# An FFN's wide gate and up groups on TensorE: contraction tiles outside and product kinds inside, or the other way round

## The reference, cut to what matters

```
def swiglu(x, w_gu, w_dn):
    g, u = jnp.split(x @ w_gu, 2, axis=-1)
    return (jax.nn.silu(g) * u) @ w_dn
...
        h = h + swiglu(rmsnorm(h, norm_ffn[l]), w_gate_up[l], w_down[l])
```

## Time and profile before

| | |
|---|---|
| time, median of 3 runs | 2611.77 us (2611.46 to 2612.14) |
| the profiled execution's own time | 2613.04 us |
| its span, first to last instruction | 2611.3 us |
| TensorE (PE) busy, 15296 matmuls | 2575.4 us, 99% |
| weight loads (PEld) busy, 15296 | 2511.1 us, 96% |
| VectorE, ScalarE, GpSimd busy | 1107.2, 673.1, 675.1 us |
| mean granted TensorE clock | 0.996 |

### The profile page before, as it was taken

How to read it: one execution, slowest core, us unless ns; L and a number is a source line. 1 busy time by engine, 2 the same in 40 slices (tenths; PEclk the granted TensorE clock), 3 DMA queues, 4 the chain that set the end, 5 groups by cost and what they waited for, 6 DMA issues and landing times. The chain is left out here.

```text
span 2611.3 us, 37891 instructions
## 1 busy us (share of the span) xinstructions
PE 2575.4 (99%) x15296; PEld 2511.1 (96%) x15296; DVE 1107.2 (42%) x2301; ACT 673.1 (26%) x1474; POOL 675.1 (26%) x641
## 2 busy tenths in 40 slices
PE   8999999999999999999999999999999999999998
PEld 7999999999999999999999988899999999999998
DVE  6444464254323333332338656655333233333334
ACT  5222233142111111111115555534111111111112
POOL 1322222212221211122126343434121112211114
PEclk9999999999999999999999999999999999999999
DMA  4445555111111111111112234011111111111111
GB/s 148 142 133 143 166 172 165 49 33 41 49 41 41 42 41 48 33 49 41 41 61 42 55 81 119 18 41 49 41 43 42 46 33 49 44 42 45 41 41 73
DMA packets 244240, 171.23 MB, mean 66 GB/s; under 512 B 47352, under 2 KB 232876, under 8 KB 244036
## 3 DMA queue, kind: packets, MB, share of 16 engines
q1 hardware_dynamic: 243876, 168.78, 22.2%
q10 hardware_dynamic: 192, 0.04, 0.0%
HBM read 136.99 MB, written 33.59 MB: 65 GB/s over the span
## 5 line engine op out<-in xcount | busy, mean ns | idle before, releaser
L197 POOL TENSOR_TENSOR wl<-raw,wh 128x512 fp32r<-128x512 f32 x264 | 337.6, 1303 | 1288.4 <-ACT wh L189 1288.4
L349 PE MATMUL psum<-xh,wl 128*128 128x400 f32 (+1 forms) x1872 | 430.1, 338 | 0.0
L349 PE MATMUL psum<-xl,wh 128*128 128x400 f32 (+1 forms) x1872 | 428.5, 337 | 0.0
L349 PE MATMUL psum<-xh,wh 128*128 128x400 f32 (+1 forms) x1872 | 427.3, 336 | 0.0
L477 DVE TENSOR_TENSOR h<-h,psum 128x384 f32<-128x384 f32 (+1 forms) x528 | 265.0, 553 | 280.0 <-PE psum L369 267.2
L349 PEld LDWEIGHTS psum<-xh,wl 128*128 128x128 f32 x1872 | 336.7, 188 | 0.0
L349 PEld LDWEIGHTS psum<-xl,wh 128*128 128x128 f32 x1872 | 336.6, 188 | 0.0
L349 PEld LDWEIGHTS psum<-xh,wh 128*128 128x128 f32 x1872 | 335.9, 188 | 0.0
L2201 PE MATMUL psum<-xh,wh 128*128 128x384 f32 (+1 forms) x792 | 276.6, 349 | 8.0 <-DVE h L2373 4.8
L2201 PE MATMUL psum<-xl,wh 128*128 128x384 f32 (+1 forms) x792 | 272.2, 344 | 0.0
L2201 PE MATMUL psum<-xh,wl 128*128 128x384 f32 (+1 forms) x792 | 270.9, 342 | 0.0
(11 more groups left out here) (248 smaller groups left out, 3698.0 us busy)
## 6 DMA issues: line engine op xcount, KB each, us to landing
raw<-in_w_gate_up SPq DMA_DIRECT2D x88, 512.0 KB, 3.9
raw<-in_w_down SPq DMA_DIRECT2D x44, 512.0 KB, 3.5
raw<-in_a_w_in SPq DMA_DIRECT2D x24, 512.0 KB, 4.8
fr_qkv<-qkv_d SPq DMA_DIRECT2D x36, 256.0 KB, 3.8
qkv_d<-fr_tmp SPq DMA_DIRECT2D x32, 192.0 KB, 2.0
hn_d<-fr_hn_turned SPq DMA_DIRECT2D x36, 128.0 KB, 3.3
fr_xin<-in_x_prompt SPq DMA_DIRECT2D x8, 512.0 KB, 5.3
fr_decode_state<-in_state_c SPq DMA_DIRECT2D x4, 1024.0 KB, 7.2
```

The costliest lines, as they stand in the source:

```text
L197: pool.tensor_tensor(wl[:, self.slot(p), v], raw[:, self.raw_of(p), v], wh[:, self.slot(p), v].bitcast(F32), ALU.subtract).then_inc(self.w ...
L349: y = pe.matmul(psum[:, bank + c, 0:nt], w[:, k, :], x[:, k, t0:t0 + nt], start=(k == 0 and m == 0), stop=(k == KD - 1 and m == 2))
```

## The change

The loops over `k` and over the three kinds change places in `gate_up_wide`. The chunk stays the innermost loop. All 72 matmuls of a group are the same ones as before, with the same operands, banks, first and last accumulation flags and increments.

```
--- before.py
+++ after.py
@@ -343,8 +343,8 @@
         def gate_up_wide(p, bank):
             pe.wait_ge(self.w_lo, self.z["w_lo"] + 2 * (p + 1))
             hi, lo = weight_tile(wh[:, self.slot(p), :]), weight_tile(wl[:, self.slot(p), :])
-            for k in range(KD):
-                for m, (w, x) in enumerate(((hi, xh), (hi, xl), (lo, xh))):
+            for m, (w, x) in enumerate(((hi, xh), (hi, xl), (lo, xh))):
+                for k in range(KD):
                     for c, (t0, nt) in enumerate(tok):
                         y = pe.matmul(psum[:, bank + c, 0:nt], w[:, k, :], x[:, k, t0:t0 + nt],
                                       start=(k == 0 and m == 0), stop=(k == KD - 1 and m == 2))
```

## The result

The changed kernel takes 2619.05 us (median of 9 runs), the one before 2611.46 us in the same rounds: a ratio of 1.0029, with a 95% interval of 1.0019 to 1.0038. The change makes the kernel slower by 7.6 us. The forecast was 2615.0 us within 2609 to 2623. The time lies in the range. Its ratio is over the bound of 0.2% that I had drawn for "no difference" (the interval begins just under it, at 0.19%), so it lies in the field of the rival to which I had given 0.33.

What follows compares the result with a forecast made beforehand. TensorE, busy without gaps at full clock in the wide groups, was taken as the bound. Steps of k in layer 1 (+2.3 us) and layer 0 (+0.9) made +3.2 us, so 2615.0 us on the 2611.8 median, range 2609 to 2623.

Steps and rivals of the forecast that it cites:

- the rival to which I had given 0.33: Line 349's matmuls run at the narrow gate groups' rate: +7.0 and +5.9 us, 2624.7 us; layer 1 alone 2618.8; chance 0.33.
- What bounds the kernel: In both stretches of wide groups TensorE is always busy at full clock, so each nanosecond of a matmul counts.
- Waits, increments, loads: Wide groups: waits and increments keep their places, other engines have slack, no weight load is added or removed; no cost.
- One sign of being wrong: The forecast would be wrong if, among other signs, the down projections changed their time too; 25.22 and 25.38 us were expected.
- The stationary tile: Wide groups: eight more tile changes at 5.5 ns would make 3.4 us over 78 groups; this price was not taken.
- Steps of k, layer 1: Layer 1's wide groups: sixteen more steps of k at 3.6 ns cost 58 ns a group, +2.3 us; bounds -1.1 to +7.0.
- Layer 0: Layer 0's wide groups: +3.4 us if steps of k cost, -1.7 if column jumps do; the middle, +0.9 us, taken.
- The sum: Both layers' wide groups together: 2.3 + 0.9 = +3.2 us, giving 2615.0 us, +0.12%.
- The comparison with N / 2.4 + 2.5 ns: For 384 columns the formula gives 162.5 ns against 173.3 to 176.2 in the trace, leaving some 11 ns a matmul.
- The two ports: TensorE reads columns and weight loads independently, so loads take nothing from running matmuls; cited for the no-difference side, chance 0.22.
- the rival without any effect: Read order in wide groups makes no difference, 2611.8 us, or the excess goes entirely, 2609.0 us; chance 0.22.
- P: Follow-up explanation, not in the forecast: a matmul is held up when its columns' start address modulo 256 bytes changes.

Runs made afterwards that it cites:

- the kinds innermost: Against the kernel before: k outside, then the chunk, then the kinds inside, so the stationary tile changes at 48 of 72 matmuls; 2615.46 us in one execution.
- the place outside: Against the change: loops over the columns' start address modulo 256 bytes outermost, then kind, then k = a and a + 4, then chunk; 2613.84 us, ratio 1.0009.

## Why the prediction was right or wrong

**What bounds the kernel** was right. TensorE has no gap in the two stretches, and each nanosecond between starts reached the end: 6.8 us of longer groups are 6.8 us of span.

**Waits, increments, loads** at no cost: right. No wait appeared in the two stretches, counts and load times stayed. One sign of being wrong that the prediction had named did come, in small: the wide down projections of layer 1 changed their time, by 15 ns each.

**The stationary tile** at no price: right for layer 1, and the kernel with the kinds innermost showed it directly. The 5.5 ns worked out from narrow and wide groups was the price of something else in which these differ.

**Steps of k, layer 1**: the mechanism was right and its size wrong. The term was +2.3 us, and it measured 6.25 us. The step that failed is the choice among the three bounds: "the wide form is nearer in all but that one point". That one point, a step of `k` every three matmuls, was the one that counted. I had the row with the same rhythm and named it as the upper bound; groups behind another group came to within 0.1 ns a matmul of it. I had priced every step alike, at 3.6 ns. A step cost (12.507 - 12.480) / 8 = 3.4 ns in the old order and (12.680 - 12.480) / 24 = 8.3 ns in the new one.

The steps aren't alike even within a group. At the floor three matmuls take 520 ns. In the old group the three triples behind each of four places in a row differ from that by -5.0, 0, 0; -4.2, +12.5, +2.5; -3.4, 0, 0; and +10.8, 0, 0 ns, in all 13 ns, and the next four places repeat it. In the new group, one triple to a place, it is +10.9, +1.7, +17.4 and +3.3 ns, 33 ns for four places, six times over. That the next place comes before the rhythm has settled fits this, but it isn't shown as the reason. In the old order with `xl` moved by 64 bytes the place moves 16 times, at distances of three and six matmuls, and a move costs 53 / 16 = 3.3 ns, no more than in the old layout. With the place outside the rhythm doesn't settle within 18 matmuls: behind one of the four moves the six triples are off by +5.4, +4.9, +2.4, +1.5, +5.1 and +6.0 ns.

**Layer 0**: the middle of +3.4 and -1.7 was +0.9, measured +0.4 us. The number is near, but neither of the two rules behind it held: a group in the steady run has the same 12.680 us in both orders, and the 0.4 us stands at the ten groups behind a down projection. That is luck more than insight.

**The sum**: +3.2 us, measured +6.8 in the span and +7.6 between the medians, whose interval reaches from 0.19 to 0.38%. The rival "behaves as the narrow gate groups do", for layer 1 alone, had 2618.8 us and was the right one. I should have given it more than the forecast. The comparison with N / 2.4 + 2.5 ns in the prediction leaves something out: the Trainium skill (TensorE: Matmul & The Clock Gate, "Back-to-back issue gap") gives that formula for isolated matmuls and says that in a stream of weight loads and matmuls both set the spacing. So the 11 ns by themselves don't speak against it.

**The two ports.** By the Trainium skill (TensorE: Matmul & The Clock Gate, "Step-by-step: what each phase is for") the columns and the weight loads are read through two independent ports, so that a load takes nothing from a running matmul. Nothing in layer 1 speaks against that: 48 changes of the tile in a group and not 16 left it at 12.507 us. What failed is my step from there to "the order makes no difference". The rule says nothing of the start address of the columns, and by order and layout the same 72 matmuls took 12.480 to 12.680 us.

**What stays open.** Shown is that in the gate, up and wide down groups of layer 1 the time over the floor comes with changes of the columns' place modulo 256 bytes: where the place was held constant, groups behind one another ran at the floor, the gate and up groups in either order. Not shown is why, nor what a change costs. Over the floor, a wide group paid 200 ns for 24 changes, 53 for 16, 40 for 12, 27 for 8, 60 for 4 and 20 for 2, so the number of changes doesn't give the price.

Nor does every change cost. The narrow down projection of the earlier trace rows reads hidden tiles whose parts lie 36 x 256 + 128 bytes apart with rows of 18 x 256 + 64 bytes. Counted from the first one, its place modulo 256 bytes goes 0, 128, 0, 64, 192, 64, another at every matmul, and it runs at 173.3 ns all the same (in layer 1 too: 1.040 us for six by the starts, where nothing comes between). The wide down projection of layer 1 reads the same tiles with three matmuls at each place and took 257 ns over its floor. The prediction had named this row as speaking for the rival without any effect, and P as stated above doesn't explain it.

I can't say either which hardware resource it is, why the place outside was slower than the old order, or what sets layer 0's times, where a chunk of 400 columns is not a whole number of 256-byte pieces (1600 bytes) and changes the place by itself. A rule that gives all the group times measured here wasn't found.

## What to carry to other kernels

Where TensorE is the bound, read the distance between starts, by group, and compare groups with equal columns; here that showed differences of 1.6% that no busy time, no idle time and no wait shows. Give the rows that TensorE streams a length that is a multiple of 256 bytes, and put tiles that are read in turn at distances that are multiples of it; with 384 columns that brought the wide groups here to their floor. If that isn't to be had, measure the orders, since fewer changes of place weren't always better (60 ns for 4, 27 ns for 8). And look at what the layout costs elsewhere: here a later load took back more than the floor gave. When a sum needs an estimate, start from the row that shares the feature which the change alters, even if it differs in everything else.

## What the runs showed of the hardware that I had not expected

- The starts are repeatable to a nanosecond: in all kernels with the old order and the old layout the group of layer 1 took 12.505 to 12.508 us behind another.
- The start address of the moving columns can have a price. With 384 columns, a 128x128 tile and fp32r operands a matmul of a wide group takes 173.33 ns where the place modulo 256 bytes stays, and on average 176.1 ns where it moves on by 64 bytes every three matmuls. Moving it by 256 bytes with each change of kind cost nothing (12.480 us a group); moving it by 64 bytes cost 53 ns a group at 16 moves. The narrow down projection, whose place moves at every matmul, ran at 173.3 ns.
- A change of place isn't a fixed price on one matmul. The triples behind it came from 5 ns early to 18 ns late; in the old order they were back at 520 ns within nine matmuls, with the place outside not within 18, and the mean price of a change ran from 3.3 to 15 ns.
